# Gated DeltaNet heads: GpSimd's elementwise products behind the last row move of a level, and the turned blocks of up to 32 rows made by VectorE in SBUF

## What is computed

```python
k_beta = k * beta[..., None]
lmat = jnp.where(strict, jnp.einsum('bhnck,bhnsk->bhncs', k_beta, k) * decay, 0.0)
a = lmat + jnp.eye(CHUNK, dtype=jnp.float32)
rhs = jnp.concatenate([v * beta[..., None], k_beta * jnp.exp(g)[..., None]], axis=-1)
sol = lax.linalg.triangular_solve(a, rhs, left_side=True, lower=True, unit_diagonal=True)
u, w = sol[..., :DV], sol[..., DV:]
attn = jnp.einsum('bhnck,bhnsk->bhncs', q, k) * decay
```

## Time and profile before

| | before |
|---|---|
| median of 3 runs | 2577.07 us |
| the profiled execution | 2576.94 us |
| its span in the profile | 2575.2 us |
| PE busy (share of the span) | 2382.1 us (93%) |
| DVE busy | 1052.7 us (41%) |
| ACT busy | 933.4 us (36%) |
| GpSimd busy | 268.0 us (10%) |
| one head of the loop | 146.2 us |

### The profile page before, as it was taken

The page is one execution under the profiler, slowest core; times in us unless marked ns, Lnnn a source line. Parts: engine busy times, 40 slices in busy tenths (PEclk is TensorE's granted clock), DMA queues, the critical chain, the costliest instruction groups (busy, mean ns, idle before and its releaser), DMA issues.

```text
span 2575.2 us, 39585 instructions
## 1 busy us (share of the span) xinstructions
PE 2382.1 (93%) x14398; PEld 1735.0 (67%) x14398; DVE 1052.7 (41%) x2052; ACT 933.4 (36%) x2443; POOL 268.0 (10%) x196
## 2 busy tenths in 40 slices
PE   6879999999999999999899999919999999999994
PEld 3455656566565656665555554419999999999994
DVE  2457574756657574764624431660100100010012
ACT  3154544536354544635431103312222223223212
POOL 0011110211011110211100000000110101011000
PEclk8989999999999999999999999959999999999997
DMA  9511212020121202011342322265788688778864
GB/s 324 216 44 36 66 26 76 1 73 28 36 66 27 75 25 76 1 37 57 103 159 106 120 71 98 90 230 206 250 294 298 236 281 300 265 261 291 302 224 156
DMA packets 196567, 362.53 MB, mean 141 GB/s; under 512 B 8922, under 2 KB 70311, under 8 KB 193355
## 3 DMA queue, kind: packets, MB, share of 16 engines
q1 hardware_dynamic: 190027, 341.77, 38.1%
q0 software_dynamic: 6400, 18.88, 3.0%
HBM read 319.97 MB, written 40.65 MB: 140 GB/s over the span
## 4 chain that ended last, share of the span: by engine, by line
PE 84%; DVE 9%; issue 3%; ACT 2%; DMA 2%; DVEq 0%; SPq 0%; POOL 0%; ACTq 0%; POOLq 0%
PE bank L610 27%; PE bank L2052 20%; PE bank L2066 10%; PE bank L1487 5%; PE bank L1732 5%; DVE arena L1112 3%; PE bank L1505 2%; PE bank L796 2%; PE bank L865 1%; PE bank L854 1%; PE bank L870 1%; PE bank L788 1%; PE bank L845 1%; PE bank L869 1%; DVE arena L1117 1%
## 5 line engine op out<-in xcount | busy, mean ns | idle before, releaser
L610 PE MATMUL bank<-arena 128*128 128x512 f32 (+1 forms) x2496 | 927.3, 497 | 17.8 <-DMA arena<-in_w_in 16.2
L2052 PE MATMUL bank<-arena 128*128 128x144 f32 x4096 | 514.0, 286 | 5.1 <-ACT arena L2085 5.1
L2052 PEld LDWEIGHTS bank<-arena 128*128 128x128 f32 x4096 | 510.7, 190 | 5.3 <-ACT arena L2085 5.3
L610 PEld LDWEIGHTS bank<-arena 128*128 128x128 f32 x2496 | 374.6, 192 | 169.9 <-issue 168.0
L2134 DVE TENSOR_TENSOR arena<-arena,bank 128x144 f32<-128x144 f32 x128 | 39.0, 304 | 707.7 <-ACT arena L2093 707.7
L2066 PE MATMUL bank<-arena 128*128 128x144 f32 x2048 | 257.2, 286 | 0.7 <-DVE arena L2134 0.7
L2066 PEld LDWEIGHTS bank<-arena 128*128 128x128 f32 x2048 | 253.8, 189 | 1.9 <-DVE arena L2134 0.9
L796 PEld LDWEIGHTS bank<-arena 128*128 128x128 f16 x1296 | 97.7, 98 | 188.9 <-issue 155.4
L2093 ACT ACTIVATE arena<-bank 128x144 f32<-128x144 f32 x128 | 37.3, 291 | 465.4 <-PE bank L2052 465.4
L970 ACT ACTIVATE arena<-bank 128x384 f16<-128x384 f16 (+1 forms) x360 | 161.7, 496 | 121.9 <-PE bank L796 79.3
L641 ACT ACTIVATE arena<-bank 128x512 f32<-128x512 f32 (+1 forms) x156 | 76.6, 491 | 217.3 <-PE bank L610 216.8
(11 more groups left out here) (274 smaller groups left out, 2640.6 us busy)
## 6 DMA issues: line engine op xcount, KB each, us to landing
arena<-in_exp_w_gate SPq DMA_DIRECT2D x32, 2048.0 KB, 10.1
arena<-in_exp_w_up SPq DMA_DIRECT2D x32, 2048.0 KB, 15.5
arena<-in_exp_w_down SPq DMA_DIRECT2D x32, 2048.0 KB, 10.8
arena<-in_w_in SPq DMA_DIRECT2D x52, 512.0 KB, 5.6
arena<-in_ada_w SPq DMA_DIRECT2D x24, 1024.0 KB, 7.5
side_dram<-arena SPq DMA_DIRECT2D x20, 576.0 KB, 3.6
arena<-side_dram SPq DMA_DIRECT2D x20, 576.0 KB, 3.9
arena<-g_dram SPq DMA_DIRECT2D x16, 576.0 KB, 5.4
```

Of the source, the lines that this page charges most:

```text
L610: ins = nc.tensor.matmul(unit_bank(order, name)[:, 0:n], w[:, k, :], hT3[:, k, at:at + n], start=(k == 0), stop=(k == KD - 1))
L2052: last = nc.tensor.matmul(banks[3 + f % 2][:, m * CAP:(m + 1) * CAP], w_unit[2 * half + m][:, k, col:col + P], xsT[:, k, :], start=(k == 0 ...
```

## The change

Five edits, all in the heads.

1. After the moves of levels 2, 4, 8 and 16 DVE turns each group of `up` into `up_turned` in SBUF (`turn_blocks`, a transpose of 32 x 32 blocks; `up` holds only diagonal blocks of at most 32 then). PE's transposes at levels 4, 8, 16 and 32 and ACT's copies of them are gone; only level 64 keeps them. At P of levels 4 to 32 PE waits for `up_turned`. ACT, which had been held back by the copies, now waits for `up_changed` before it overwrites `low_old`.
2. GpSimd's four long operations wait for the last `to_up` of levels 4, 8, 16 and 32, and go in the order `nLlo[0]`, `attnT[0]`, `nLlo[1]`, `attnT[1]`.
3. GpSimd's six selects wait for all of `X_init`, DVE's copies under a mask (L1091).
4. ACT's `halves` stand one level earlier.
5. `FILLS`: 6 in place of 3 at `start`, and 2 in place of 1 at P of group 2 in levels 2, 4, 8 and 16; `end2` is left with 4 in place of 11.

```diff
-        USES[1] += ["Y2"] + [f"{x}{b}" for b in LEVELS for x in ("XP" if b > LEVELS[0] else "P")]
+        USES[1] += ["Y2"] + [f"{x}{b}" for b in LEVELS for x in ("XP" if b == LEVELS[-1] else "P")]
...
-        FILLS = {"start": 3, "nk": 5, "qT": 16, "kk": 16, "Y20": 8, "Y21": 8, "Y22": 2, "X0": 1, "X1": 1, "X2": 1, "res": 2, "fix": 4, "end1": 6}
-        FILLS |= {f"{x}{b}_{g}": 1 for b in LEVELS for x in "ZP" for g in range(3)}
+        FILLS = {"start": 6, "nk": 5, "qT": 16, "kk": 16, "Y20": 8, "Y21": 8, "Y22": 2, "X0": 1, "X1": 1, "X2": 1, "res": 2, "fix": 4, "end1": 6}
+        FILLS |= {f"{x}{b}_{g}": 1 for b in LEVELS for x in "ZP" for g in range(3)} | {f"P{b}_2": 2 for b in LEVELS[:-2]}
...
                     products(0, f"Z{b}", g, [(both, low)])
-                    if lv > 0:
+                    if b == LEVELS[-1]:
                         pe.wait_ge(sem("up_changed"), changed(h, lv - 1, g))
                         turn(1, f"X{b}", up, g)
                     fill(f"Z{b}_{g}")
                 for g in range(3):
+                    if 0 < lv < len(LEVELS) - 1:
+                        pe.wait_ge(sem("up_turned"), turned_count(h, lv - 1, g))
...
                     copy(0, f"Z{b}", Zc, g)
+                    if b == LEVELS[-1]:
+                        copy(1, f"X{b}", up_turned, g, F16)
                     if lv > 0:
-                        copy(1, f"X{b}", up_turned, g, F16)
+                        act.wait_ge(sem("up_changed"), changed(h, lv - 1, g))
                         keep(g)
                     evac(f"Z{b}_{g}")
-                    if lv in (1, 2, 3) and g < 2:
-                        halves(2 * (lv - 1) + g)
+                    if lv < 3 and g < 2:
+                        halves(2 * lv + g)
...
+                def turn_blocks(g):
+                    if lv < len(LEVELS) - 2:
+                        dve.wait_ge(sem("up_changed"), changed(h, lv, g))
+                        alone(dve)
+                        nc.vector.transpose(flat(up_turned, g), flat(up, g)).then_inc(sem("up_turned"), 1)
+
                 join(0)
                 to_low(0)
                 join(1)
                 to_up(0)
                 to_low(1)
+                turn_blocks(0)
                 join(2)
                 to_up(1)
                 to_low(2)
+                turn_blocks(1)
                 to_up(2)
+                turn_blocks(2)
...
-                    pool.wait_ge(sem("triangles"), 8 * h + g + 6)
+                    pool.wait_ge(sem("X_init"), 6 * h + 6)
...
+            all_drained(pool, h, 1, "kq")
             for d in range(2):
-                all_drained(pool, h, 1, f"P{LEVELS[1 + 2 * d]}")
+                pool.wait_ge(sem("up_changed"), changed(h, 1 + 2 * d, 2))
                 pool.wait_ge(sem("nL_ready"), 6 * h + 3 * d + 3)
                 nc.gpsimd.tensor_tensor(nLlo[d], Yf[d], nL[d], ALU.subtract).then_inc(sem("nLlo_ready"), 1)
-            for d in range(2):
-                all_drained(pool, h, 1, f"P{LEVELS[4 + d]}")
+                pool.wait_ge(sem("up_changed"), changed(h, 2 + 2 * d, 2))
                 pool.wait_ge(sem("decay_masked"), 2 * h + d + 1)
-                all_drained(pool, h, 1, "kq")
                 nc.gpsimd.tensor_tensor(attnT[d], kq[1], dm[d], ALU.mult).then_inc(sem("attn_ready"), 1)
```

More of the change, by code:

```diff
@@ L893, in changed, with turned_count @@
             return 3 * (len(LEVELS) * h + lv) + g + 1
+        def turned_count(h, lv, g):
+            return 3 * ((len(LEVELS) - 2) * h + lv) + g + 1
         def flat(x, g):
```

## The result

The changed kernel takes 2554.42 us (median of 4 runs, 2553.6 to 2556.36), the kernel before in the same comparison 2576.96 (4 runs, 2576.8 to 2578.41). The ratio is 0.9912, 95% interval 0.9895 to 0.993: 22.5 us or 0.9% faster, where 29.2 us were forecast. The profiled execution took 2555.21 us with a span of 2553.5.

The account below looks back on a forecast made before the run. PE was taken to bound the kernel, idle 4.15 us a head in the levels behind DVE moves held by GpSimd. 7 x (2.56 + 0.6 + 0.44) + 4.0 = 29.2 us off 2576.94 gave 2547.7 us, range 2530 to 2566.

Parts of the forecast that it names:

- The sign: Whole kernel: the change makes it faster, chance 0.87, against same 0.06 and slower 0.07.
- leading mechanism: Levels: PE loses 12 groups of transposes, 2.0 us a head; most stall time only moves from L1112 to the tap.
- The levels: Levels of each loop head: 51.41 us against 50.53, with 3.44 of fills moved in, so a gain of 2.56 us.
- taps are not held: Rival, levels: products do not delay taps, PE sets all levels, 4.8 us a head more gone, 2514 us; chance 10%.
- The dear transpose: Rival, levels: DVE transposes take 0.94 us each, costing 2.3 us a head, 2563 us; 17% together with the held transpose.
- the held transpose: Rival, levels: transposes take 0.56 us but GpSimd's product must wait for the third, 2559 us; 17% with the dear transpose.
- Ahead of the levels: Just before the levels: selects no longer run beside L1091, so PE's wait of 1.0 us shrinks by 0.6 a head.
- The joint: Between two heads: 1.08 us hidden by the fills of `start`, less a new 0.64 wait for `o_normed`, net 0.44.
- The number of heads: Sum over heads: seven equal heads, each gaining 2.56 + 0.6 + 0.44 us, plus 4.0 for the last.
- The last head: Last head, no taps: products fall into idle DVE time, waits mostly go; gain 4.0 us, between 2 and 6.6.
- Slower: Rival, levels 4, 8 and 16: transposes both dear and excluding GpSimd, 5.1 us more a head, 2583 us; chance 7%.

## Why the prediction was right, and where it was off

The sign, the range and the leading mechanism held; 6.7 us of the 29.2 were missing. The terms that were too large are those of the joint, of the first head and of the last.

- **The levels** gained 50.53 + 3.44 - 51.50 = 2.47 us a head, forecast 2.56. The steps behind it are each seen: transposes at 0.574 and every 0.49, taps held at 2.36 to 3.27, levels of 8.39, 9.29 and 8.89, a `to_low` of level 64 that is held. Two small errors cancel in levels 8 and 16: the products alone take 2.62 and 2.22 us, 0.15 more than I got from the earlier trace rows by taking off all the time until L1117 ended, but they start 5.52 us behind the join (929.79 - 924.27) and not 5.66. In level 4 the start is at 5.62, and the level is 0.11 longer than forecast. The kernel before already had a row that gives both the length and the lock: its first `nLlo` (L1240 at 921.91) starts 0.23 us behind the tap L1047 (921.68, 0.82 long) and takes 2.67, so this tap too held a product. The prediction didn't use it.
- **The rival "taps are not held"** priced the lock at 4.8 us a head, from levels of 7.40 set by PE; cutting the products gave 4.71 and levels of 7.38 (740.53 to 747.91). **The dear transpose** fell (0.574 alone and beside a product), and so did that of the held transpose.
- **Ahead of the levels** I took 0.6 of the wait of 1.0; all of it went, as the selects alone also show (1.0 a head).
- **The joint** is the step that failed. I took PE's 1.08 saved at the head's start less a new wait of 0.64, net 0.44. The 1.08 went and the new wait is 0.47, but the three fills added at `start` bring others forward, and PE reached the narrow fills of `qT` before ACT had emptied their bank: 0.93 us by its row, 1.3 in a head when taken away. I had followed the wide fills to where they end and not asked where the narrow ones then fall. What is ahead of the levels and the joint together gave 47.64 - 3.44 - 43.77 = 0.43 a head instead of 1.04; the waits account for 1.0 + 1.08 - 0.47 - 0.93 = 0.68, and 0.25 us are left that no row names.
- **The number of heads.** I took seven equal heads. The first gained about 1.6 only: its first fills behind the weights start at 144.0 us, before at 142.1, and this start scatters (147.0 with the products cut). 6 x 2.84 + 1.6 + 3.0 for the last = 21.6 against 21.7 of span.
- **The last head** gained 3.0 instead of 4.0, and the step behind that number failed. I let GpSimd's products fall into idle time of DVE and their waits mostly go. But a product starts with the last `to_up` and reaches into the next level, where it holds the first `to_low` of levels 8 to 64 (1.50, 1.72, 1.25 and 1.43 us in place of 0.56). PE waits as long for DVE's moves as before, 4.5 us against 4.6:

```profile
PE bank L797 <- DVE arena L1120: 2.2, 3, 1.2
PE bank L789 <- DVE arena L1125: 1.3, 3, 0.6
PE bank L789 <- DVE arena L1120: 1.0, 1, 1.0
```

  The longest of these, 1.24 us at 1211.83, is no held move: narrow fills stand there now, as the prediction feared for level 64, and PE comes early.
- **Slower** was given 7% by dear and excluding transposes. The kernel does become slower with some of the edits (1.0087 with the transposes alone, 1.0089 with the fills alone), but not by this step: in the kernel with the transposes alone they take 0.573 us each. What makes it slower there, a fourth held move and a wait at the joint, doesn't show with all five edits.

The edits don't add. Alone on the kernel before they give -31 (products), -6 (selects), +24 (transposes with the early halves) and +22 (fills), some +9 in sum; together they give -22.5. The transposes take DVE's slack and let the products in ahead of the taps; the fills fill the room that the transposes leave and, if the inference on queue q8 is right, need a loop body that has lost its reload.

## What to carry to other kernels

Where an instruction of VectorE and one of GpSimd exclude each other, the question is which asks first: the engine on the critical path should, even by 0.16 us, and a harmless short instruction between a shared wait and the critical one hands the lock to the other side. Better still, put GpSimd's long operations where VectorE idles. A table of filler work has to be followed to where every kind of filler falls, with who empties its bank, and an edit that pays in company should also be timed alone, since here one of five gave more than all five.

## What was not expected

- A float16 transpose of 128x384 on VectorE takes 574 ns with 0.49 us to the next start, no more than a move under a mask (556), and neither holds a GpSimd product nor is held by one.
- The order of two instructions at a level's end moves 18.5 us.
- PE's busy time for the same 746 matmuls was 138.56 us with seven waits in a head and 137.21 with two. It is no fixed amount for each wait: in the kernel with the products alone, five waits fewer than before lowered it by 0.21 only (139.95 to 139.74).
- Queue q8, which loads instructions, falls from 90 packets to 35 with 36 fewer matmuls in the loop's head, and in the one kernel that still loads and has only four fills in `end2`, the joint shows 2.5 to 3.0 us of wait.
- In four of the kernels (the transposes alone, the fills alone, all but the fills, three fills moved) the granted clock falls for a short stretch in some heads of the loop and not in others (0.98 or 0.99 over the head), and the heads of one kernel are then up to 2.2 us apart.
